# Token tiles stationary and 512 weight columns moving, in the FFNs and output projections of a three-layer network on one core

## The chip, the cores and the metric

The kernel runs on one core of a Trainium2 chip. The metric is the device time of one execution in microseconds (us). The profiled execution is a separate one, taken by the hardware profiler.

## The reference, cut to what matters

256 tokens of 1024 features go through three layers: a matrix memory mixer (mixa), a windowed attention mixer (mixb) and a state-space mixer (ssd). There are five FFNs of 2816 hidden columns: before and after mixa, before and after mixb, and after ssd. All is float32.

```
def rms_norm(x, g):
    y = xf * lax.rsqrt(jnp.mean(xf * xf, axis=-1, keepdims=True) + EPS)
    return y * g
def swiglu(x, w_in, w_out):
    gate, up = jnp.split(x @ w_in, 2, axis=-1)
    return (jax.nn.silu(gate) * up) @ w_out
mem_kv = rms_norm(mem, mem_norm_g) @ mem_w_kv
for i in range(2):
    x = x + 0.5 * swiglu(rms_norm(x, ffn1_norm_g[i]), ffn1_w_in[i], ffn1_w_out[i])
    proj = rms_norm(x, mix_norm_g[i]) @ w_in
    x = x + concat(token_mixer(proj), memory_heads(proj)) @ w_out
    x = x + 0.5 * swiglu(rms_norm(x, ffn2_norm_g[i]), ffn2_w_in[i], ffn2_w_out[i])
h = x + hybrid_mixer(rmsnorm(x, norm_mix_w))          # ends with merged @ w_o
h = h + (silu(hn @ w_gate) * (hn @ w_up)) @ w_down    # hn = rmsnorm(h, norm_ffn_w)
return rmsnorm(h, final_norm_w)
```

## The kernel before, in words

**Units of weights.** Every weight matrix comes in units of 1 MB (128 partitions x 2048 elements). A g unit is 8 k-tiles (128 input features each) of 256 output columns. A d unit is 2 k-tiles (256 input rows) of 1024 output columns. Three slots (RING) hold the units in turn. SP's queue loads unit u into w_raw when VectorE has split unit u-3 (`load`). ScalarE rounds it to float32r, w_hi (`round_`, L553), when TensorE has used unit u-3 (w_used). VectorE writes the remainder w_lo = w_raw - w_hi (`split`, L966). Activations are held as such a pair too (xg_hi and xg_lo, y_hi and y_lo), and every product is made in three passes: hi x hi, hi x lo, lo x hi.

**Matmuls.** In `block_passes` (L1676 to 1678) a 128x128 block of weights is the stationary operand and the 256 tokens are the moving one. The output is one of the 128-row blocks of features, by token. A unit has 48 such matmuls. A g unit fills one PSUM bank, (4, 5 or 6 in turn, `bank`), and a d unit adds into banks 0 to 3, which stay open over a whole FFN or projection.

**The FFN.** 11 steps (NI) of 256 hidden columns. A step is three units: g of gate, g of up, d of the step before. VectorE takes gate and up out of their banks and scales them by rstd, a row of the 256 tokens' 1/rms held on all partitions (`evac`, L1038). ScalarE makes the silu (L605), VectorE the product (L1054), ScalarE and VectorE its hi and lo (L609, L1058), which are the moving operand of the next d unit. The middle steps are in a hardware loop, two a turn.

**The residual and the norms.** x is held by feature: 8 tiles of 128 features x 256 tokens. The last d unit of a stage frees the banks 0 to 3 in order. VectorE adds them to x (L993), ScalarE scales x by the next norm's gain and rounds it (xg_hi, L575), VectorE makes xg_lo (L975), two tiles at a time, and the first g unit of the next stage takes them k-tile by k-tile. ScalarE squares x (L564), GpSimd adds the squares (L502), and two float32 matmuls with a matrix of ones bring the sum of each token on all partitions (`stat`, L1715 and 1716). The root (`token_root`) is Ln and Exp on ScalarE and a step of refinement on VectorE (L1017 to 1027), on 128x256 tiles. The root is applied only when a product is taken out of its bank. ScalarE loads a table of functions before it (ACT_TABLE_LOAD) and another one after it, for the silu.

**The ends.** mem and x come in by token and are turned by 16 transposes each (`turn`, L1723). At the end x times the final gain is turned back (L2134), and 32 records of matmuls with one moving column give the sums of squares (L2139).

**Order of the work.** Each engine has its own list, written out by hand, and waits on semaphores. In one engine's list an operation that waits holds all behind it. Of an FFN's entrance VectorE's list is: norm, split(u+2), split(u+3), token_root, evac of gate, product; u is the first unit of the FFN.

Of the kernel before, what the change touches and what calls it, by code (L numbers as in the profile page):

```python
# [17 lines left out]
F32 = mybir.dt.float32  # L18
# [6 lines left out]
P = 128  # L25
T = 256
# [33 lines left out]
def plan_units():  # L60
# [7 lines left out]
    ffn = "gg" + "ggd" * (NI - 1) + "d"  # L68
# [23 lines left out]
def build(nc, a, out, known=None):  # L92
# [6 lines left out]
    with ExitStack() as ctx:  # L99
# [10 lines left out]
        x = sb("x", [P, DT, T])  # L110
# [5 lines left out]
        rs_v = sb("rs_v", [P, T])  # L116
        rs_y = sb("rs_y", [P, T])
        rs_t = sb("rs_t", [P, T])
# [32 lines left out]
        sq = tiles(KB(0, 8), 512)  # L151
        gate_s, up_s = KB(8, 2), KB(10, 2)
        xin = tiles(KB(16, 8), D)
        memin = tiles(KB(24, 8), D)
        x_gain = tiles(KB(8, 8))
        fin_r, fin_v, fin_t = small[:, 0:2], small[:, 2:4], small[:, 4:6]
        mem_t = tiles(KB(8, 8))
        yout = tiles(KB(16, 8), D)
# [12 lines left out]
        turned = sem("turned")  # L171
        x_new = sem("x_new")
        xh_ready, xl_ready = sem("xh_ready"), sem("xl_ready")
        squared, sq_summed, stat_done = sem("squared"), sem("sq_summed"), sem("stat_done")
        rs_vec, rs_act = sem("rs_vec"), sem("rs_act")
        ffn_silu, ffn_h, ffn_hh, ffn_hl = (sem(n) for n in ("ffn_silu", "ffn_h", "ffn_hh", "ffn_hl"))
# [3 lines left out]
        def g_src(w, c):  # L180

            return w.rearrange("(k p) c -> p k c", p=P)[:, :, bass.ds(c, 256)]

        def d_src(w, r):

            return w[bass.ds(r, 256), :].rearrange("(k p) c -> p k c", p=P)

        FFNS = [(a["ffn1_w_in"][0], a["ffn1_w_out"][0]), (a["ffn2_w_in"][0], a["ffn2_w_out"][0]),
                (a["ffn1_w_in"][1], a["ffn1_w_out"][1]), (a["ffn2_w_in"][1], a["ffn2_w_out"][1]), None]

        def ffn_src(f, kind, i):

            if f == 4:
                w = {"g": a["w_gate_2"][0], "u": a["w_up_2"][0], "d": a["w_down_2"][0]}[kind]
                return d_src(w, i * 256) if kind == "d" else g_src(w, i * 256)
            w_in, w_out = FFNS[f]
            if kind == "d":
                return d_src(w_out, i * 256)
            return g_src(w_in, i * 256 + (FF if kind == "u" else 0))
# [23 lines left out]
        vector("final", r128(a["final_norm_w_2"]), 8)  # L223
# [13 lines left out]
        def col(name, k=0):  # L237
# [8 lines left out]
                  ("final", "final", 1.0)]  # L246
        LAST = ([p[0] for p in PHASES if p[0].startswith("ffn")] or [""])[-1]
        norm_of = {p[0]: (n, p[1], p[2]) for n, p in enumerate(PHASES)}

# [92 lines left out]
        def _(sp):  # L342
# [4 lines left out]
            def load(u, src, i=0):  # L347
# [5 lines left out]
                sp.dma_start(w_raw[:, u % RING, :].rearrange("p (k c) -> p k c", k=src.shape[1]),  # L353
                             src).then_inc(w_landed[u % RING], 16)

            def ffn(f):
                u = U[f"ffn{f}"]
                load(u, ffn_src(f, "g", 0))
                load(u + 1, ffn_src(f, "u", 0))
                for i in (1, 2):  # L360
                    load(u + 3 * i - 1, ffn_src(f, "g", i))
                    load(u + 3 * i, ffn_src(f, "u", i))
                    load(u + 3 * i + 1, ffn_src(f, "d", i - 1))
                with sp.Fori(0, (NI - 3) // 2) as n:
                    for j in range(2):
                        i, v = 3 + j, u + 8 + 3 * j
                        load(v, ffn_src(f, "g", 2 * n + i), n)
                        load(v + 1, ffn_src(f, "u", 2 * n + i), n)
                        load(v + 2, ffn_src(f, "d", 2 * n + i - 1), n)
                load(u + 3 * NI - 1, ffn_src(f, "d", NI - 1))  # L370
# [14 lines left out]
            def mem():  # L385
                for j in range(3):
                    load(U["mem"] + j, g_src(a["mem_w_kv"], 256 * j))
                sp.dma_start(xin, a["x"][0].rearrange("(k p) d -> p k d", p=P)).then_inc(x_loaded, 16)
# [45 lines left out]
            for c in range(4):  # L434
                if c % 2:
                    sp.wait_ge(act_done, act_.at(f"out {c}"))
                else:
                    sp.wait_ge(vec_done, vec.at(f"out {c}"))
                tt, f = c // 2, slice(512 * (c % 2), 512 * (c % 2) + 512)
# [5 lines left out]
        def _(pool):  # L445
# [49 lines left out]
            def norm(n):  # L495

                pool.wait_ge(squared, 4 * n + 2)
                for c in range(1, 4):
                    if c > 1:
                        pool.wait_ge(squared, 4 * n + c + 1)  # L500
                        pool.wait_ge(sq_summed, 3 * n + c - 1)
                    pool.tensor_tensor(sq[:, 0], sq[:, 0], sq[:, c], ALU.add).then_inc(sq_summed, 1)  # L502

# [32 lines left out]
            for name, _, _ in PHASES[:-1]:  # L536
                norm(norm_of[name][0])
# [5 lines left out]
        def _(act):  # L543
            roots = [0]

            def round_(u, i=0):
# [3 lines left out]
                act.wait_ge(w_landed[u % RING], 16 * (u // RING + 1) + 32 * i)  # L550
# [8 lines left out]
            def norm(n, gain, split=True):  # L559
                src = x if n else mem_t  # L560

                def squares():
                    for c in range(4):
                        act.activation(sq[:, c], src[:, 2 * c:2 * c + 2], ACT.Square).then_inc(squared, 1)  # L564

                if n == 1:
                    act.wait_ge(stat_done, 1)
                    act.wait_ge(x_new, 8)
                    squares()
                    act.wait_ge(w_used, U["ffn0"])  # L570
                for c in range(4):
                    act.wait_ge(x_new, 4 * n + c + 1)
                    if split:
                        for k in (2 * c, 2 * c + 1):
                            act.activation(xg_hi[:, k], src[:, k], ACT.Identity, scale=col(gain, k)).then_inc(xh_ready, 1)  # L575
                if n == 0:
                    round_(1)
                if n != 1:
                    squares()
# [11 lines left out]
            def ffn(f, n, gain):  # L591
                u = U[f"ffn{f}"]
                norm(n, gain)
                round_(u + 2)
                round_(u + 3)
                if f == 0:
# [3 lines left out]
                root(rs_y[:, :], rs_v[:, :])  # L600
                act.preload_act_table_set(SETS["silu"])

                def silu(v, i, it=0):
                    evacuated(v, it)
                    act.activation(gate_s, gate_s, ACT.Silu).then_inc(ffn_silu, 1)  # L605

                def product(i, p):
                    act.wait_ge(ffn_h, NI * nth[f] + i + 1)
                    act.activation(y_hi[:, 2 * p:2 * p + 2], tiles(up_s), ACT.Copy).then_inc(ffn_hh, 1)  # L609

                def step(g, i, p, it=0):
                    round_(g + 2, it)
                    silu(g, i, it)
                    round_(g + 3, it)
                    product(i, p)
                    round_(g + 4, it)

# [1552 lines left out]
```

## Time and profile before

| | |
|---|---|
| median of 3 runs | 1721.25 us (1720.28 to 1721.38) |
| profiled execution | span 1719.2 us, 31086 instructions |
| TensorE (PE) busy | 1652.2 us |
| VectorE (DVE) busy | 1089.0 us |
| ScalarE (ACT) busy | 792.4 us |
| GpSimd (POOL) busy | 182.1 us |
| mean granted TensorE clock | 0.989 of full speed |
| HBM | 275.01 MB read, 161 GB/s over the span |

For the profiled execution no time beside its span is given. PE is a matmul, PEld a load of the stationary operand. A record's length of a matmul includes its way through the array, so in a stream records overlap, and the distance of their starts is what a matmul costs. A float32 matmul stands in the trace as two records, a float32r one and a transpose as one.

How the rows below are to be read. The timeline: start in us, length in us (for "x10" from the first start to the last end of ten records), engine, line, operation, out<-in, shape, and in brackets idle time before and what ended it. The windows: the stretch, its length, busy us and records of PE, PEld, DVE, ACT and POOL, then the granted clock (1.00 is 2.4 GHz, 0.50 is 1.2 GHz), the busy share of the DMA engines and GB/s. The groups of instructions by line: busy us in all, mean ns of one, and idle time before them with its releaser.

### The profile page before, as it was taken

The page shows a single profiled execution, that of the slowest core. Times are in us where ns is not written, and L with a number is a line of the kernel's source. Part 1 is how long each engine was busy: PE and PEld are TensorE (multiplying, and loading weights), DVE is VectorE, ACT ScalarE, POOL GpSimd, SP SyncE. Part 2 cuts the span into 40 slices and gives each one's busy share as a digit, 9 for nine tenths or more (in the row PEclk, how much of TensorE's full clock was granted, in tenths as well). Part 3 has the DMA queues.
Part 4 walks back from the last instruction along what each step waited for, and adds up shares of the span by engine and source line. Part 5 has one row for each costly group of instructions (what it writes and reads, how often), then busy time and mean ns, then how long its engine had stood idle before and what let it go on. Part 6 is the DMA issues. An engine that isn't in the chain of part 4 may idle for free. (4 is left out here: it accounts for less than half of the span.)

```text
span 1719.2 us, 31086 instructions
## 1 busy us (share of the span) xinstructions
PE 1652.2 (96%) x13337; PEld 1615.0 (94%) x13337; DVE 1089.0 (63%) x1237; ACT 792.4 (46%) x892; POOL 182.1 (11%) x137
## 2 busy tenths in 40 slices
PE   6999999999999999999999999997889999999998
PEld 6999999999999999999789999996789999999998
DVE  5565566576665665556676655689777756665554
ACT  5543353455434453436556434454446534453432
POOL 2100010011000010001301000056741000010000
PEclk9999999999999999999999999998999999999999
DMA  8355555434555555555223555544224655545551
GB/s 251 124 183 184 195 153 167 137 110 154 187 196 172 194 172 184 183 179 170 92 87 118 199 186 176 190 148 141 80 76 150 204 184 182 183 151 197 172 194 49
DMA packets 218181, 277.42 MB, mean 161 GB/s; under 512 B 4972, under 2 KB 198888, under 8 KB 218088
## 3 DMA queue, kind: packets, MB, share of 16 engines
q1 hardware_dynamic: 218088, 276.08, 49.3%
q8 instruction: 71, 1.16, 0.3%
q14 instruction: 22, 0.18, 0.0%
HBM read 275.01 MB, written 1.05 MB: 161 GB/s over the span
## 5 line engine op out<-in xcount | busy, mean ns | idle before, releaser
L966 DVE TENSOR_TENSOR w_lo<-w_raw,w_hi 128x2048 fp32r<-128x2048 f32 x260 | 602.8, 2320 | 385.4 <-ACT w_hi L553 385.1
L1676 PE MATMUL ps<-xg_hi,w_hi 128*128 128x256 f32 x2888 | 830.4, 288 | 16.3 <-DVE xg_lo L975 11.9
L1677 PE MATMUL ps<-xg_lo,w_hi 128*128 128x256 f32 x2888 | 820.4, 284 | 0.0
L1678 PE MATMUL ps<-xg_hi,w_lo 128*128 128x256 f32 x2888 | 820.2, 284 | 0.0
L553 ACT ACTIVATE w_hi<-w_raw 128x2048 fp32r<-128x2048 f32 x260 | 494.6, 1905 | 190.1 <-PE ps L1678 176.2
L1676 PEld LDWEIGHTS ps<-xg_hi,w_hi 128*128 128x128 f32 x2888 | 557.5, 193 | 24.3 <-DVE w_lo L966 9.5
L1677 PEld LDWEIGHTS ps<-xg_lo,w_hi 128*128 128x128 f32 x2888 | 557.6, 193 | 0.5
L1678 PEld LDWEIGHTS ps<-xg_hi,w_lo 128*128 128x128 f32 x2888 | 557.4, 193 | 0.0
L1676 PE MATMUL ps<-y_hi,w_hi 128*128 128x256 f32 x1264 | 358.8, 284 | 4.8 <-DVE y_lo L1355 2.8
L1677 PE MATMUL ps<-y_lo,w_hi 128*128 128x256 f32 x1264 | 357.7, 283 | 0.0
L1678 PE MATMUL ps<-y_hi,w_lo 128*128 128x256 f32 x1264 | 357.6, 283 | 0.0
L1676 PEld LDWEIGHTS ps<-y_hi,w_hi 128*128 128x128 f32 x1264 | 242.6, 192 | 6.5 <-DVE y_lo L1355 3.3
L1677 PEld LDWEIGHTS ps<-y_lo,w_hi 128*128 128x128 f32 x1264 | 242.6, 192 | 0.0
L1678 PEld LDWEIGHTS ps<-y_hi,w_lo 128*128 128x128 f32 x1264 | 242.6, 192 | 0.0
L502 POOL TENSOR_TENSOR scr<-scr 128x512 f32<-128x512 f32 x27 | 54.0, 1999 | 1098.8 <-ACT scr L564 1096.2
L1038 DVE SCALAR_TENSOR_TENSOR scr<-ps,rstd 128x512 f32<-128x512 f32 x141 | 96.6, 689 | 86.4 <-PE ps L1678 86.0
L605 ACT ACTIVATE scr<-scr 128x512 f32<-128x512 f32 x55 | 34.7, 632 | 218.0 <-DVE scr L1038 218.0
L609 ACT ACTIVATE y_hi<-scr 128x512 fp32r<-128x512 f32 x55 | 34.8, 632 | 209.4 <-DVE scr L1054 209.4
L1058 DVE TENSOR_TENSOR y_lo<-scr,y_hi 128x512 fp32r<-128x512 f32 x55 | 38.1, 692 | 38.4 <-ACT y_hi L609 38.4
L1465 DVE SCALAR_TENSOR_TENSOR mem_v<-mem_k,cols,mem_v 128x255 f32<-128x255 f32 (+2 forms) x72 | 46.5, 709 | 0.0
L515 POOL TENSOR_SCALAR mem_k<-mem_k 128x512 f32<-128x512 f32 x12 | 39.9, 3326 | 47.2 <-ACT mem_k L857 47.2
L575 ACT ACTIVATE xg_hi<-x,cols 128x256 fp32r<-128x256 f32 x64 | 28.0, 500 | 31.5 <-DVE x L993 26.6
(292 smaller groups left out, 948.9 us busy)
## 6 DMA issues: line engine op xcount, KB each, us to landing
w_raw<-in_ffn_w_in_dram SPq DMA_DIRECT2D x88, 1024.0 KB, 5.1
w_raw<-in_ffn_w_out_dram SPq DMA_DIRECT2D x44, 1024.0 KB, 4.9
w_raw<-in_w_in_dram SPq DMA_DIRECT2D x41, 1024.0 KB, 5.3
w_raw<-in_a_w_in_dram SPq DMA_DIRECT2D x15, 1024.0 KB, 5.3
w_raw<-in_w_gate_dram SPq DMA_DIRECT2D x11, 1024.0 KB, 5.3
w_raw<-in_w_up_dram SPq DMA_DIRECT2D x11, 1024.0 KB, 5.3
w_raw<-in_w_down_dram SPq DMA_DIRECT2D x11, 1024.0 KB, 4.9
w_raw<-in_w_ssd_proj_dram SPq DMA_DIRECT2D x8, 1024.0 KB, 5.3
```

The lines of the kernel that those rows point to most:

```text
L502: pool.tensor_tensor(sq[:, 0], sq[:, 0], sq[:, c], ALU.add).then_inc(sq_summed, 1)
L515: pool.tensor_scalar(s_in[:, q:q + 2], s_in[:, q:q + 2], 1.0, None, ALU.add).then_inc(pool_done, pool_(f"S th {c}"))
L553: act.activation(w_hi[:, u % RING, :], w_raw[:, u % RING, :], ACT.Copy).then_inc(w_rounded, 1)
L605: act.activation(gate_s, gate_s, ACT.Silu).then_inc(ffn_silu, 1)
L609: act.activation(y_hi[:, 2 * p:2 * p + 2], tiles(up_s), ACT.Copy).then_inc(ffn_hh, 1)
L966: dve.tensor_tensor(w_lo[:, s, :], w_raw[:, s, :], w_hi[:, s, :].bitcast(F32), ALU.subtract).then_inc(w_split, 1)
L1038: dve.scalar_tensor_tensor(out=dst, in0=tiles(ps[:, bank(u), :]), scalar=scale, in1=wide(rstd[:, :] if r is None else r), op0=ALU.mult, op ...
L1058: dve.tensor_tensor(y_lo[:, 2 * p:2 * p + 2], tiles(up_s), y_hi[:, 2 * p:2 * p + 2].bitcast(F32), ALU.subtract).then_inc(ffn_hl, 1)
L1465: dve.scalar_tensor_tensor(out=s_cv[:, q + t, s:], in0=s_in[:, q + t, 0:T - s], scalar=col(f"conv_w{tap_}", conv_tile(c) + t), in1=s_cv[:, ...
L1676: pe.matmul(dst, hi, xh, start=start, stop=False, skip_group_check=True)
L1677: pe.matmul(dst, hi, xl, start=False, stop=False, skip_group_check=True)
L1678: last = pe.matmul(dst, lo, xh, start=False, stop=stop, skip_group_check=True)
```

## The change

**Operands exchanged.** In the FFNs, in both `mix*_out` projections and in w_o the stationary operand is now a 128x128 tile of tokens by features (xg or y, hi or lo), and the moving one is 512 columns of the weight unit (`row_passes`). A unit has 24 matmuls of 512 columns in place of 48 of 256. All other products stay as they were.

**Units.** A step of the FFN is still three units, but gate and up are mixed: each of the first two has 4 k-tiles, with 256 columns of gate and 256 of up side by side (`gu_src`, `gate_up`). The output [128 tokens x (256 gate, 256 up)] of the two token tiles is in banks 4 and 5. There is one such pair of banks; the next step's first unit waits for ffn_h in the first step, and in the loop comes behind a wait for it. Every unit is now loaded by two DMAs.

**Hidden values.** ScalarE makes the silu straight from the bank, scaled by rcol, the root as a column [128 tokens x 2]; VectorE makes the product from the bank with the same scale into h_s, by token. Four transposes (`hidden`) turn it into bank 6, from which hi and lo are made. `hidden(i)` stands in the middle of the d unit of step i-1 (after its second quarter), and for step 0 between the first and second unit of step 1.

**Residual.** x is held by token ([128, 2, 1024]). The d unit goes by quarters (token tile, half of the columns): (0,0), (1,0), (0,1), (1,1). At the end of a stage TensorE turns each added quarter by four transposes into two banks (`turn`), ScalarE and VectorE make xg_hi and xg_lo out of these banks. The turns of the first two quarters lie inside the last d unit, the others inside the first unit of the next stage.

**Norms.** ScalarE squares x by token tile and sums in its accumulator (`square`), the root is taken on two columns. The squares' sum on GpSimd and the two `stat` matmuls are gone. In the mixers two matmuls turn the root's columns into the row rstd (`token_row`). At the end the final gain is loaded as a row, and no transposes are made.

**Lists at the FFN's entrance.** ScalarE's: round u+1, four tiles of xg_hi, round u+2, square, four tiles, square, root, silu table, wait for the root, round u+3, silu. VectorE's: three adds, four tiles of xg_lo, last add, split(u+1), four tiles, split(u+2), token_root, split(u+3), product(0).

The diff, cut to its core:

```
-    ffn = "gg" + "ggd" * (NI - 1) + "d"
+    ffn = "d" * (3 * NI)
-        x = sb("x", [P, DT, T])
+        x = sb("x", [P, 2, D])
...
+        QUARTERS = ((0, 0), (1, 0), (0, 1), (1, 1))
+        def quarter(tt, half):
+            return ps[:, 2 * half + tt, :]
...
+            def high(n, gain, half_):
+                for k in range(4 * half_, 4 * half_ + 4):
+                    act.wait_ge(turned, 2 * n + half_ + 1)
+                    act.activation(normed_of(n)[0][:, k], block_of(n, k), ACT.Identity, scale=col(gain, k)).then_inc(xh_ready, 1)
+            def square(n, tt):
...
+                act.activation(sq_out[:, tt], (x if n else memin)[:, tt], ACT.Square, accum_out=ssq[:, tt:tt + 1]).then_inc(squared, 1)
+            def norm(n, gain, u):
+                round_(u + 1)
+                high(n, gain, 0)
+                round_(u + 2)
+                square(n, 0)
+                high(n, gain, 1)
+                square(n, 1)
...
-                root(rs_y[:, :], rs_v[:, :])
+                root(rn_y, rn_v)
                 act.preload_act_table_set(SETS["silu"])
+                act.wait_ge(rs_vec, root_.at(f"norm {n}") + 3)
+                round_(u + 3)
+                def silu(g, i, it=0):
+                    act.wait_ge(ffn_gu, NI * nth[f] + i + 1)
+                    act.activation(gate_s[:, 0], ps[:, 4, 0:256], ACT.Silu, scale=rcol[:, 0:1]).then_inc(ffn_silu, 1)
+                    act.wait_ge(w_used, g + 2 + 6 * it)
+                    act.activation(gate_s[:, 1], ps[:, 5, 0:256], ACT.Silu, scale=rcol[:, 1:2]).then_inc(ffn_silu, 1)
+                def step(g, i, p, it=0, first=False):
                     round_(g + 2, it)
+                    if first:
+                        hidden_high(0, 0)
+                    round_(g + 3, it)
                     silu(g, i, it)
                     round_(g + 4, it)
+                    hidden_high(i, p)
...
+            def norm(n, gain, factor, u):
+                for j in range(3):
+                    add(n, factor, u, j)
+                low(n, gain, 0)
+                add(n, factor, u, 3)
+                split(u + 1)
+                low(n, gain, 1)
+                split(u + 2)
...
+                token_root(n)
                 split(u + 3)
-                token_root(n)
+                def product(i):
+                    for tt in range(2):
+                        dve.wait_ge(ffn_silu, 2 * (NI * nth[f] + i) + tt + 1)
+                        dve.scalar_tensor_tensor(out=h_s[:, tt], in0=ps[:, 4 + tt, 256:512], scalar=rcol[:, tt:tt + 1], in1=gate_s[:, tt],
+                                                 op0=ALU.mult, op1=ALU.mult).then_inc(ffn_h, 1)
...
+            def row_passes(dst, xh, xl, s, at, start, stop):
+                hi, lo = w_hi[:, s, at:at + 512], w_lo[:, s, at:at + 512]
+                pe.matmul(dst, xh, hi, start=start, stop=False, skip_group_check=True)
+                pe.matmul(dst, xh, lo, start=False, stop=False, skip_group_check=True)
+                return pe.matmul(dst, xl, hi, start=False, stop=stop, skip_group_check=True)
...
+            def gate_up(u, half_, it=0, norm=None, first=None):
+                s = u % RING
+                pe.wait_ge(w_split, u + 1 + 6 * it)
+                for tt in range(2):
+                    if first is not None:
+                        pe.wait_ge(ffn_h, first + tt)
+                    for k in range(4):
+                        kt = 4 * half_ + k
+                        if norm is not None and tt == 0:
+                            pe.wait_ge(xl_ready, 8 * norm + kt + 1)
+                        tok = slice(tt * P, tt * P + P)
+                        last = row_passes(ps[:, 4 + tt, :], xg_hi[:, kt, tok], xg_lo[:, kt, tok], s, 512 * k, kt == 0, kt == 7)
+                    if half_ and tt == 0:
+                        last.then_inc(ffn_gu, 1)
+                    if norm is not None and norm > 1 and half_ == 0 and tt == 0:
+                        turn(norm, 2)
+                        turn(norm, 3)
+                last.then_inc(w_used, 1)
...
+                for j, (tt, h) in enumerate(QUARTERS):
+                    tok = slice(tt * P, tt * P + P)
                     for k in range(2):
+                        last = row_passes(quarter(tt, h), yh[:, y0 + k, tok], yl[:, y0 + k, tok], s, k * D + 512 * h,
+                                          start and k == 0, k == 1)
+                    if norm is not None and j < 3:
                         last.then_inc(acc_ready, 1)
+                    if norm is not None and norm < len(PHASES) - 1 and j in (1, 2):
+                        turn(norm, j - 1)
+                    if hidden and j == 1:
+                        hidden()
...
+                def hidden(i):
+                    pe.wait_ge(ffn_h, 2 * (NI * nth[f] + i) + 2)
+                    for fb in range(2):
+                        for tt in range(2):
+                            last = pe.transpose(ps[:, 6, fb * T + tt * P:fb * T + tt * P + P], h_s[:, tt, fb * P:fb * P + P], ident[:, :])
+                    last.then_inc(ffn_ht, 1)
```

## Rows read from the trace of the kernel before

**Rows 1.** Page, busy us and share of the span by engine:
```profile
PE 1652.2 (96%) x13337; PEld 1615.0 (94%) x13337; DVE 1089.0 (63%) x1237; ACT 792.4 (46%) x892; POOL 182.1 (11%) x137
```
**Rows 2.** Windows, all engines: inside an FFN, and the start of ssd:
```profile
500.00:550.00 50.00, 50.00 (x419) 50.00 (x418) 27.49 (x20) 20.36 (x15) 0.00 (x0) 1.00 0.56 188
1150.00:1200.00 50.00, 38.03 (x282) 36.66 (x281) 48.07 (x71) 24.86 (x35) 30.40 (x13) 0.87 0.46 146
```
**Rows 3.** Timeline (start, length) inside an FFN, PE and PEld:
```profile
456.56 0.28 PE L1676 MATMUL ps<-xg_hi,w_hi 128*128 128x256 f32 x1
456.56 0.19 PEld L1677 LDWEIGHTS ps<-xg_lo,w_hi 128*128 128x128 f32 x1
456.68 0.28 PE L1677 MATMUL ps<-xg_lo,w_hi 128*128 128x256 f32 x1
```
**Rows 4.** Timeline, PE: float32 records of 256, 512 and 1 columns:
```profile
347.05 2.32 PE L1801 MATMUL ps<-mem_k,scr 128*128 128x256 f32 x10
...
847.07 1.45 PE L1917 MATMUL ps<-scr,rotate 128*128 128x512 f32 x3
...
1709.15 3.63 PE L2139 MATMUL ps<-ones,scr 128*128 128x1 f32 x32
```
**Rows 5.** Timeline, PE, in a stretch at half clock:
```profile
14.38 0.41 PE L1676 MATMUL ps<-xg_hi,w_hi 128*128 128x256 f32 x1
14.59 0.41 PE L1677 MATMUL ps<-xg_lo,w_hi 128*128 128x256 f32 x1
```
**Rows 6.** Timeline, PE: sixteen transposes in a row:
```profile
316.31 1.91 PE L1865 MATMUL ps<-ident,scr 128*128 128x128 f32 x16
```
**Rows 7.** Groups by line: the first of the two statistic matmuls:
```profile
L1715 PE MATMUL ps<-scr,ones 128*128 128x256 f32 x18 | 5.5, 385 | 0.3 <-POOL scr L502 0.3
```
**Rows 8.** Timeline at a boundary from one FFN to the next:
```profile
595.97 1.71 ACT L575 ACTIVATE xg_hi<-x,cols 128x256 fp32r<-128x256 f32 x4 [2.96 <-DVE x L993]
...
596.48 0.28 PE L1678 MATMUL ps<-y_hi,w_lo 128*128 128x256 f32 x1
597.15 0.36 PE L1676 MATMUL ps<-xg_hi,w_hi 128*128 128x256 f32 x1 [0.39 <-DVE xg_lo L975]
...
599.31 1.66 DVE L975 SCALAR_TENSOR_TENSOR xg_lo<-x,cols,xg_hi 128x256 fp32r<-128x256 f32 x4
```
**Rows 9.** Groups by line: ScalarE's and VectorE's operations (busy, mean ns of one):
```profile
L553 ACT ACTIVATE w_hi<-w_raw 128x2048 fp32r<-128x2048 f32 x260 | 494.6, 1905 | 190.1 <-PE ps L1678 176.2 <-DMA w_raw<-in_mem_w_kv_dram 13.6
L585 ACT ACT_TABLE_LOAD x18 | 23.1, 1283 | 0.3
L587 ACT ACTIVATE scr<-scr 128x1024 f32<-128x1024 f32 x2 | 2.1, 1060 | 2.3 <-DVE scr L1017 2.3
L666 ACT ACTIVATION_READ_ACCUMULATOR scr<-ps,small 128x1 f32 x16 | 3.3, 209 | 0.0
...
L966 DVE TENSOR_TENSOR w_lo<-w_raw,w_hi 128x2048 fp32r<-128x2048 f32 x260 | 602.8, 2320 | 385.4 <-ACT w_hi L553 385.1
L1023 DVE SCALAR_TENSOR_TENSOR rs_t<-rs_t,rs_v 128x256 f32<-128x256 f32 x9 | 3.8, 424 | 0.3
```
**Rows 10.** Timeline: first and last VectorE record of a root on two columns:
```profile
1712.82 0.16 DVE L1017 TENSOR_SCALAR small<-ps 128x2 f32<-128x2 f32 x1 [4.00 <-PE ps L2139]
...
1713.88 0.16 DVE L1027 SCALAR_TENSOR_TENSOR small<-small 128x2 f32<-128x2 f32 x1
```
**Rows 11.** Windows: a stop of TensorE, and the stretches behind two stops:
```profile
20.70:23.60 2.90, 0.24 (x3) 0.04 (x1) 1.24 (x1) 0.00 (x0) 2.76 (x2) 0.99 0.99 185
23.50:26.90 3.40, 3.26 (x15) 3.26 (x16) 0.00 (x0) 0.41 (x1) 0.97 (x1) 0.50 1.10 362
...
866.80:870.00 3.20, 3.20 (x16) 2.87 (x17) 3.20 (x14) 1.88 (x4) 0.00 (x0) 0.50 0.27 104
```
**Rows 12.** Timeline: the last matmul of the last d unit, and the stores:
```profile
1705.59 0.28 PE L1678 MATMUL ps<-y_hi,w_lo 128*128 128x256 f32 x1
...
1714.86 1.83 SPq L440 DMA_DIRECT2D out_dram<-scr  x4
```

More of the change, by code:

```diff
@@ L592, in ffn @@
                 u = U[f"ffn{f}"]
[L593 to L596, printed above, removed]
+                if f:
+                    norm(n, gain, u)
+                else:
+                    for tt in range(2):
+                        square(n, tt)
+                    round_(u + 2)
                     for j in range(2):
@@ L636, in ffn @@
                     step(u + 11 + 6 * (bodies - 1), NI - 1, 0)
-                round_(u + 3 * NI + 1)
             def mem(n, gain):
                 u = U["mem"]
-                norm(n, gain)
+                act.wait_ge(vec_done, vec.at("mem gain"))
+                high(n, gain, 0)
+                round_(u + 1)
+                high(n, gain, 1)
+                for tt in range(2):
+                    square(n, tt)
                 round_(u + 2)
+                root(rn_y, rn_v)
                 round_(u + 3)
-                root(rs_y[:, :], rs_v[:, :])
-                round_(u + 4)
+                for half_ in range(2):
+                    high(n + 1, PHASES[1][1], half_)
                 for j in range(2):
@@ L1076, in step @@
                         next(extra, None)
-                evac(tiles(gate_s), u)
-                product(u, 0)
-                low(0, 0)
-                step(u + 2, 1, 1, more=f == 1)
+                product(0)
+                step(u + 2, 1, 1, more=f == 1, first=True)
                 if f == 0:
@@ L1687, in g_unit @@
                     pe.wait_ge(drained[s], fills[u] - 1 + 2 * i)
-                for n, off in enumerate(offs):
-                    for k in range(8):
-                        if norm is not None and n == 0:
-                            pe.wait_ge(xl_ready, 8 * norm + k + 1)
-                        if ready and n == 0:
-                            ready(k)
-                        last = block_passes(ps[:, b, n * T:n * T + T], s, k * 256 + off, xh[:, kt0 + k],
-                                            xl[:, kt0 + k], opens and n == 0 and k == 0, k == 7)
@@ L1696, in g_unit @@
-                last.then_inc(w_used, 1)
-            def d_unit(u, i=0, Y=None, y0=0, start=False, norm=None):
+                order = [(n, off, k) for n, off in enumerate(offs) for k in range(8)]
+                if norm is not None:
+                    order = [(n, off, k) for h in range(2) for n, off in enumerate(offs) for k in range(4 * h, 4 * h + 4)]
+                for n, off, k in order:
+                    if norm is not None and n == 0:
+                        if k == 4:
+                            turn(norm, 2)
+                            turn(norm, 3)
+                        pe.wait_ge(xl_ready, 8 * norm + k + 1)
+                    if ready and n == 0:
+                        ready(k)
+                    last = block_passes(ps[:, b, n * T:n * T + T], s, k * 256 + off, xh[:, kt0 + k],
+                                        xl[:, kt0 + k], opens and n == 0 and k == 0, k == 7)
@@ L1727, in ffn, with token_row @@
+            def token_row(n):
+                pe.wait_ge(rs_vec, root_.at(f"norm {n}") + 3)
+                for tt in range(2):
+                    last = pe.matmul(ps[:, STAT, tt * P:tt * P + P], rcol[:, tt:tt + 1].broadcast_to([P, P]), ident[:, :], start=True, stop=True)
+                last.then_inc(stat_done, 1)
             def ffn(f, n):
                 u = U[f"ffn{f}"]
-                g_unit(u, norm=n)
+                if f == 0:
+                    for v in range(u - 3, u):
+                        evacuated(v)
+                gate_up(u, 0, norm=n)
@@ L2123, in _ @@
             pe.wait_ge(mem_loaded, 16)
-            turn(memin, 0)
+            pe.wait_ge(vec_done, vec.at("mem gain"))
+            for j in range(2):
+                turn(0, j)
             for name, _, _ in PHASES:
@@ L2130, in _ @@
                     {"mem": mem, "mixa": mixa, "mixb": mixb, "ssd": ssd}[name](n)
-            for k in range(DT):
-                pe.wait_ge(vec_done, vec.at(f"x gain {k}"))
-                for tt in range(2):
-                    last = pe.transpose(ps[:, 2 * tt + k // 4, (k % 4) * P:(k % 4) * P + P], x_gain[:, k, tt * P:tt * P + P], ident[:, :])
-            last.then_inc(pe_done, pe_("out"))
-            pe.wait_ge(squared, 4 * norm_of["final"][0] + 4)
-            for tt in range(2):
-                for k in range(DT):
-                    last = pe.matmul(ps[:, STAT, tt:tt + 1], tiles(sq[:, k // 2])[:, k % 2, tt * P:tt * P + P], ones[:, 0:1],
-                                     start=k == 0, stop=k == DT - 1, skip_group_check=True)
-            last.then_inc(stat_done, 1)
     return {e: c.found for e, c in counts.items()}
```

451 lines of the change are left out of this document (209 added, 242 removed).

## The prediction, made before the change was run

> **What bounds the kernel now.** I read the busy shares first: TensorE is busy for 1652.2 us of the span of 1719.2 us, VectorE for 63% and ScalarE for 46% [rows 1]. The windows show where: in a stretch inside an FFN (500 to 550 us) TensorE is busy for all 50 us at the full clock while VectorE has 27.5 us and ScalarE 20.4 us; only the start of the last mixer (1150 to 1200 us) is a VectorE stretch, 48.1 us of 50 [rows 2]. So for an FFN the question is how densely matmuls follow each other. A matmul record lasts 284 ns, but that is its way through the array; the timeline shows the next one starting 0.12 us later, 456.56 and 456.68, and so on [rows 3]. 256 columns at 2.4 GHz are 106.7 ns, so 13.3 ns of each 120 are not streaming. Two things could be behind it, and they decide this case. Rows with one moving column settle it as far as this trace can: 32 records in 3.63 us, so (3.63 - 0.25) / 31 = 0.109 us each, with nothing to stream [rows 4]. That is the loading of 128 stationary columns. In the stream a load record starts with the matmul before it and its own matmul starts 0.12 us later [rows 3]. And at half clock, where 256 columns take 213.3 ns, the spacing is 0.21 us with no addition [rows 5]: the load is hidden there. I read 120 ns as the interval of a load, not of a matmul.
>
> **The matmuls.** The five FFNs have 33 weight units each and the output projections 6 + 6 + 4; each unit has 48 matmuls of 256 columns, so 181 x 48 = 8688, at 0.120 us 1042.6 us. After the change there are 4344 of 512 columns, each again with one load. No float32r matmul of 512 columns stands in the trace. The nearest rows are float32 passes, which stand at two array cycles a column: ten records of 256 columns in 2.32 us are (2.32 - 0.38) / 9 = 0.216 us for 512 cycles, and 512 columns take (1.45 - 0.59) / 2 = 0.43 us for 1024 [rows 4]. Both are the streaming plus 2 to 3 ns, with a load hidden in each. I take 0.216 us: 938.3 us, a gain of 104.3. Bounds: 0.2133 (streaming alone, 12 us better) and 0.240 (twice the row of now, no gain at all).
> The row for 256 columns is 120 ns [rows 3]. By the Trainium skill ("TensorE: Matmul & The Clock Gate", section "Wait — 56ns, not 53.3ns?") a warm matmul starts N/2.4 GHz plus about 2.5 ns after the last. That is 109 ns for 256 columns, against the trace, and 215.8 for 512. Were the page right for both widths, a pair would go from 218.4 to 215.8 and the edit would be worth 11 us instead of 104; the row of 120 decides against it.
>
> **Transposes that are added.** An FFN step (256 hidden columns) now has h by token and turns it back: four 128x128 transposes, 5 x 11 x 4 = 220. Sixteen of them in a row take 1.91 us, (1.91 - 0.27) / 15 = 0.109 us each [rows 6]: 24.0 us on TensorE. Lower bound the same; upper bound 0.272 us each, a record's whole length, if four alone between wide matmuls don't overlap. The residual must be turned for each norm too: 16 transposes at 7 boundaries (mem and x were turned before as well), 112 x 0.109 = 12.2 us.
> The Trainium skill ("TensorE: Matmul & The Clock Gate", section "Part 4: PE-mode transpose") gives some 275 ns for a transpose in a kernel. As a record's length the trace agrees (272 ns); as the price in a row it has 109. With 275 for all 332 the two items would be 91 us instead of 36 and the change a loss of 5; rival E below is its case here, worked out from the 272 of the row.
>
> **Norms.** The sum of squares leaves TensorE (ScalarE's accumulator makes it): 9 stages x 4 records of 256 columns in float32 x 0.216 = 7.8 us less [rows 7]. Four mixer stages get 4 records of 128 columns (broadcasting the root), 0.11 us each, 1.8 us. Net -6.0.
>
> **Boundaries.** Now TensorE stops three times at the entrance of a stage, because xg_lo comes in pairs: 596.48 to 597.15 and so on, where 0.12 would do, in all 1.6 us at each of 7 boundaries [rows 8]. In the new order the last down unit runs by quarter, and the turns of the first two quarters lie inside it. The last quarter is 6 x 0.216 = 1.3 us; in it and just after it lie the drain (0.2), two scalings on ScalarE (0.43 us apart) and one xg_lo (0.45) [rows 8]: first product about 0.4 us after the last down matmul, and then 0.65 us per k-tile against 0.43 on the other engines. So an FFN boundary stalls 0.4 us instead of 1.6 (four times: -4.8). In a mixer the second half of the k-tiles comes earlier: ScalarE first rounds a weight unit (1.9) and squares 1024 elements (1.06 + 0.21) [rows 9], and only then scales; TensorE, through with its first half and eight transposes at about 4.2 us, waits until 5.8. That makes 2.2 us in mixa and mixb, 3.2 in the last one, +2.8 in all. Net -2.
>
> **Entrance of an FFN.** Here a stall is added. Gate and up of one step fill two banks, for two token tiles, and there is no second pair. So the third unit (gate_up of step 1) can't start before product(0) has read them, and product(0) needs the root and stands behind split(u+3) in VectorE's queue. With 0 at the end of the last down unit: TensorE does unit u from 0.4 to 6.5 (24 x 0.216 and 0.87 of transposes) and u+1 until 11.7. ScalarE gets the last four k-tiles turned at 4.1 and has scaled them by 5.8; VectorE's last xg_lo is out at 6.7, then split(u+2) runs 2.3 us to 9.0. The root of two columns is 1.2 us from its first VectorE record to its last [rows 10], 10.2. ScalarE loads the silu table after its Exp (1.28 us) to about 11.0, rounds u+3 (1.9) to 12.9; VectorE splits it (2.3) to 15.2; silu is done by then, the first product takes 0.45: 15.7. TensorE stands from 11.7, 4.0 us, in four FFNs; in the first, the mem values' copies take the place of the norm, 3.6 us. Together 19.6. Behind the split wait both products, h's transposes and so the bank pair. The trace also shows what such a stop costs later: after 2.9 us with TensorE nearly idle, 3.4 us at half clock (15 matmuls in 3.4 us); the same after the stop at 864.9 [rows 11]. I charge 1.5 us each, +7.5. Bounds of this item: 0, if my order of events is too strict, and 35.
>
> **Inside the loop.** A step is 72 x 0.216 + 0.44 = 16.0 us, 17.3 now. The transposes of h come after half a down unit, 12 x 0.216 = 2.6 us behind the end of gate_up; until then silu of the second tile (0.2 + 0.45) and its product (0.45) must be done: 1.2 us, slack 1.4. ScalarE has 3 x 1.9 + 1.5 us in a step, VectorE 3 x 2.3 + 1.6 (three or four short operations, 0.42 us per 256 columns) [rows 9], so both stay below TensorE. A weight unit lands and is rounded some 4 us before it is needed; two DMAs a unit instead of one cost SP 0.4 us more of 5.3. Nothing of it reaches TensorE.
>
> **Smaller ones.** First FFN: it waits for evac of the last mem unit before it opens its banks, 0.95 us, and the mem keys' root on VectorE is closer to TensorE: +2. The chain of the windowed attention in mixb swallows some of what its out units give: +1. End: now 13.6 us lie between the last matmul (1705.59) and the end, of them 16 transposes, 32 one-column records and 1.4 us of output [rows 4, 12]. After: add 0.7, gain and square 0.9, table 1.3, root 1.2, output 1.4, the stores' issue and landing (from 1714.86 to 1719.24: 4.4) with overlap about 9.5: -4.
>
> **Sum.** -104.3 + 24.0 + 12.2 - 6.0 - 2.0 + 27.1 + 2 + 1 - 4 = -50.0. The profiled execution spans 1719.2 us; the median of the runs is 1721.25, 2.0 above. 1719.2 - 50.0 + 2.0 = 1671 us.
>
> **Rivals.**
> A. The 13.3 ns are an addition to every matmul: 226.7 ns, +46.5 us, 1718. For it: all 12,000 records have it. Against: rows 4 and 5, where it is 2 to 3 ns or none. 7%.
> B. The slower side: float32r columns are fed at 0.469 ns each, so 512 take 240 ns. Then 104.3 is gone, and the transposes, stops and turns remain: 1775 us. It decides from 227.5 ns a matmul on (50 / 4344 above 216). For it: 120 / 256, and neither the half-clock rows nor the float32 passes (0.84 ns a column) are fast enough to show such a limit. Against: the records with one column take 0.109 us with nothing to feed, so a load explains the row without it. 4%.
> C. h is late at its transposes in every step; the place is the product of the second tile behind split in VectorE's queue. 0.4 us a step makes 22 us, 1693; to undo the gain it would take 0.9. For it: product stands behind a wait that ends with the unit. Against: the slack of 1.4. 6%.
> D. The entrance stall is hidden: -25 us, 1646. 7%.
> E. Four transposes between wide matmuls cost 272 ns each: 332 x 0.163 = +54, 1725. 2%.
> Mine has 74%, with its own range 1656 to 1688. The range 1650 to 1712 leaves out B, E, most of A and half of D, about 18%. A change within 0.2% can't be told from none here: faster 0.90, same 0.04, slower 0.06.
>
> **What would show it.** In the timeline of an FFN the starts of wide matmuls 0.216 us apart (0.227 is A, 0.240 is B); groups of four transposes at 0.11 with no idle ahead; a wait of TensorE for the product (ffn_h) of about 4 us once in each FFN, followed by 3.4 us at half clock; the first wait at a boundary below 0.5 us for FFNs and one of 1.6 in mixers; the tail at 9.5 us. An FFN of 33 units should go from 190 us to about 182. If waits for h stand in every step, or if the spacing isn't 0.216, the sum is wrong.

## The result, and the profile after

The changed kernel takes 1710.51 us (median of 4 runs, 1709.77 to 1711.49), the kernel before 1720.82 in the same comparison: ratio 0.9943, 95% interval 0.9931 to 0.9956. The direction is the forecast one, and the gain is clear of the noise, but of 50 us there came 10. The profiled execution spans 1708.1 us, 11.1 less than before.

The page of the changed kernel, beside [rows 1] (its matmul records fell from 13337 to 9257):

```profile
span 1708.1 us, 23310 instructions
PE 1627.5 (95%) x9257; PEld 1412.0 (83%) x9257; DVE 1000.0 (59%) x1175; ACT 806.1 (47%) x951; POOL 128.1 (7%) x110
```

TensorE is still the engine that bounds the kernel. How dense its matmuls are is read from the timeline inside an FFN, beside [rows 3], and from the windows, beside [rows 2]:

```profile
700.04 0.39 PE L1717 MATMUL ps<-w_hi,xg_hi 128*128 128x512 f32 x1
700.26 0.39 PE L1718 MATMUL ps<-w_lo,xg_hi 128*128 128x512 f32 x1
700.49 0.39 PE L1719 MATMUL ps<-w_hi,xg_lo 128*128 128x512 f32 x1
700.72 0.39 PE L1717 MATMUL ps<-w_hi,xg_hi 128*128 128x512 f32 x1
```

```profile
700.00:750.00 50.00, 50.00 (x227) 41.36 (x227) 25.06 (x18) 21.13 (x19) 0.00 (x0) 1.00 0.56 188
```

Three matmuls take 0.68 us from start to start: 0.227 us each, not 0.216. TensorE has no gap, and the load records fill 41.4 us of the 50, where they filled all 50 before.

The group of four transposes of h (an FFN's first one), and the entrance of the same FFN, where TensorE waits for the first product. The timeline, PE first, then what the other engines do in that time:

```profile
602.14 0.39 PE L1719 MATMUL ps<-w_hi,xg_lo 128*128 128x512 f32 x1
605.85 0.76 PE L1717 MATMUL ps<-w_hi,xg_hi 128*128 128x512 f32 x1 [3.32 <-DVE scr L1088]
...
614.15 0.60 PE L1812 MATMUL ps<-ident,scr 128*128 128x128 f32 x4
614.50 0.48 PE L1717 MATMUL ps<-w_hi,xg_hi 128*128 128x512 f32 x1
```

```profile
599.04 0.17 DVE L1045 TENSOR_SCALAR norms<-norms 128x2 f32<-128x2 f32 x1
599.70 1.28 ACT L627 ACT_TABLE_LOAD   x1
600.99 1.92 ACT L575 ACTIVATE w_hi<-w_raw 128x2048 fp32r<-128x2048 f32 x1
602.82 0.45 ACT L633 ACTIVATE scr<-ps,norms 128x256 f32<-128x256 f32 x1
603.01 2.29 DVE L1002 TENSOR_TENSOR w_lo<-w_raw,w_hi 128x2048 fp32r<-128x2048 f32 x1 [2.75 <-ACT w_hi L575]
605.22 0.87 DVE L1088 SCALAR_TENSOR_TENSOR scr<-ps,norms,scr 128x256 f32<-128x256 f32 x2
```

This is the chain that the prediction wrote out, link by link: root, table, rounding of u+3, its split, and only then the products, though the silu of the first token tile was ready at 603.3 and that of the second at 603.6. The windows of the stop and of what follows (the granted clock is the third number from the end):

```profile
602.20:605.80 3.60, 0.33 (x2) 0.00 (x0) 2.79 (x3) 3.23 (x4) 0.00 (x0) 0.87 0.42 147
605.80:611.60 5.80, 5.75 (x14) 4.52 (x15) 2.49 (x2) 0.00 (x0) 0.00 (x0) 0.50 0.88 292
```

14 matmuls take the time of 25: behind a stop of 3.5 us some 2.8 are lost (15 matmuls take from 605.85 to 612.06). [rows 11] had the same kind of thing, 3.4 us at half clock behind a stop of 2.9; here the stretch is twice as long.

Starts of the first matmul of a unit give the price of each stage (worked out from the timeline). A unit of gate and up takes 5.44 us (5.76 before), a down unit with its transposes 5.93, so a step 16.81 instead of 17.28. But a whole FFN of 33 units hardly changed: ffn1, ffn2 and ffn3 (after mixa, before and after mixb) took 193.7, 193.0 and 192.3 us before and take 190.7, 193.5 and 193.4 now, where the prediction had about 182.

### The profile page after: what moved, and what is told of

The parts are those of the page before. It is cut to its first block and busy times, and to the rows that moved or that the text cites. A ratio compares the mean times of both kernels' runs of the same rounds, so it can differ in the third digit from the quotient of the medians.

```text
span 1708.1 us, 23310 instructions
## 1 busy us (share of the span) xinstructions
PE 1627.5 (95%) x9257; PEld 1412.0 (83%) x9257; DVE 1000.0 (59%) x1175; ACT 806.1 (47%) x951; POOL 128.1 (7%) x110
## 5 line engine op out<-in xcount | busy, mean ns | idle before, releaser
L1717 PE MATMUL ps<-w_hi,xg_hi 128*128 128x512 f32 x912 | 361.3, 396 | 18.4 <-DVE scr L1088 16.8
L1718 PE MATMUL ps<-w_lo,xg_hi 128*128 128x512 f32 x912 | 358.6, 393 | 0.0
L1719 PE MATMUL ps<-w_hi,xg_lo 128*128 128x512 f32 x912 | 358.6, 393 | 0.0
L1709 PE MATMUL ps<-xg_hi,w_hi 128*128 128x256 f32 x1000 | 290.4, 290 | 6.6 <-DVE xg_lo L1010 4.6
L1710 PE MATMUL ps<-xg_lo,w_hi 128*128 128x256 f32 x1000 | 284.9, 285 | 0.0
L1711 PE MATMUL ps<-xg_hi,w_lo 128*128 128x256 f32 x1000 | 284.7, 285 | 0.0
L1717 PE MATMUL ps<-w_hi,y_hi 128*128 128x512 f32 x536 | 215.7, 402 | 3.0 <-DVE y_lo L1386 3.0
L1709 PEld LDWEIGHTS ps<-xg_hi,w_hi 128*128 128x128 f32 x1000 | 193.6, 194 | 11.2 <-DVE xg_lo L1010 5.3
L1710 PEld LDWEIGHTS ps<-xg_lo,w_hi 128*128 128x128 f32 x1000 | 193.8, 194 | 0.3
L1711 PEld LDWEIGHTS ps<-xg_hi,w_lo 128*128 128x128 f32 x1000 | 193.7, 194 | 0.0
```

Of the source, the lines that this page charges most:

```text
L1709: pe.matmul(dst, hi, xh, start=start, stop=False, skip_group_check=True)
L1710: pe.matmul(dst, hi, xl, start=False, stop=False, skip_group_check=True)
L1711: last = pe.matmul(dst, lo, xh, start=False, stop=stop, skip_group_check=True)
L1717: pe.matmul(dst, xh, hi, start=start, stop=False, skip_group_check=True)
L1718: pe.matmul(dst, xh, lo, start=False, stop=False, skip_group_check=True)
L1719: return pe.matmul(dst, xl, hi, start=False, stop=stop, skip_group_check=True)
```

## The experiments

In the comparisons of e2, e3 and e4 the kernel before had a median of 1719.43 us, in those of e5 and e7 1719.70, against 1720.82 in that of the change. Differences to the changed kernel (1710.51) are therefore good to a microsecond or so; each ratio is to the kernel before of its own comparison.

**e1_streams: the disputed cost by itself.** Fifteen series of 24 matmuls, each like the first of these lines (xr and wr are float32r copies, xb and wb bfloat16 ones, x and w float32):

```
for j in range(24):
    pe.matmul(ps[:, j % 4, :], xr_tile(j), wr_tile(j, 512), start=True, stop=True)
# others: accumulating in one bank; 384, 256, 128 columns; one stationary tile only;
# 64 stationary columns; bfloat16; float32; with ScalarE and VectorE streaming
```

> This kernel leaves the whole network out: it loads a piece of x and of one weight matrix, makes float32r and bfloat16 copies, and runs series of 24 matmuls on 128x128 stationary tiles, each series on a line of its own, so its time is no time of the network. Read is the distance of starts at the full clock. Theory 1, a fixed addition to each float32r matmul (13.4 ns as in the network): 512 columns 227 ns, 384 173, 256 120, 128 about 67 or the interval of a load if that is longer (112 to 120); accumulation into one bank, the same stationary tile again, and 64 stationary columns all stay at 227; bfloat16 216 and 109 at 512 and 256. Theory 2, the company of ScalarE and VectorE makes the addition: all bare float32r series of 512 columns at 216, and 227 only in the last two series, where both engines stream over SBUF. Theory 3, the part of a load that isn't hidden: 227 with 128 stationary columns, about 220 with 64.

The timeline of PE. In order: 512 columns, 384, 256, 128; 64 stationary columns; bfloat16 with 512 and 256 columns; ScalarE and VectorE streaming (L109):

```profile
23.84 5.60 PE L84 MATMUL ps<-wr,xr 128*128 128x512 f32 x24
34.72 4.35 PE L88 MATMUL ps<-wr,xr 128*128 128x384 f32 x24
38.90 3.03 PE L90 MATMUL ps<-wr,xr 128*128 128x256 f32 x24
41.77 2.80 PE L92 MATMUL ps<-wr,xr 128*128 128x128 f32 x24
49.94 5.69 PE L96 MATMUL ps<-wr,xr 128*64 128x512 f32 x24
55.47 5.35 PE L98 MATMUL ps<-wb,xb 128*128 128x512 bf16 x24
60.66 2.78 PE L100 MATMUL ps<-wb,xb 128*128 128x256 bf16 x24
77.84 5.63 PE L109 MATMUL ps<-wr,xr 128*128 128x512 f32 x24
```

Less the last record's own length and over 23: (5.60 - 0.39) / 23 = 226.6 ns for 512 columns, 174 for 384, 120 for 256. Each is the streaming at 2.4 GHz plus 13.3 (384: 14). 128 columns come out at 0.110 us, where streaming and addition would make 67 ns; rows with one column had 0.109 [rows 4], so I take this for the floor that the load sets. The bfloat16 series have 216 and 109. With 64 stationary columns nothing is saved (230). One stationary tile all the time has a median of 227 (512 columns) and 120 (256), and accumulation into one bank 227 too. In the series L109 ScalarE and VectorE stream over SBUF all the time: 228; in L84 and L86 both are silent: 226.6. So theory 1 holds, theories 2 and 3 fall: the addition is there in a kernel with nothing else in it, doesn't hang on the load, and belongs to float32r.

**e6_streams2: what carries it.** The same frame, other operands:

```
stat(j)[0:64], mov(j, 512)[0:64]          # and 0:32
stat(j), one_column.broadcast_to([128, 512])
stat(j), mov(j, 512)[:, 0::2]             # 256 columns, stride two
stat(j), mov(j, 320)
6 x wide matmul, 4 x transpose, eight times over
float32r and bfloat16 in turn
```

> Again no network, only series of 24 matmuls (float32r, 512 columns where nothing else is said), for what carries the addition of 13.3 ns: 64 and 32 rows (partitions) in place of 128; a moving operand that is one column repeated; a stationary operand that is one column repeated; 256 columns at a stride of two; 320 columns; the same moving tile each time; six wide matmuls and four transposes in turn; float32r and bfloat16 in turn. If the addition belongs to the start of a float32r matmul: 227 ns in all wide series, 120 at stride two, 147 for 320 columns, and 227 + 216 for the pair with bfloat16. If it belongs to reading a tile from memory: less with the repeated column or with few partitions. If it belongs to float32r's load of the stationary tile: gone or moved in the pair, 216 + 227 with the order of the two exchanged, and the same sum. Six wide matmuls and four transposes should take 6 x 0.227 + 4 x 0.109 = 1.80 us, and 1.85 if a group of transposes has an edge of its own, as the network's 0.49 us a group suggests.

The timeline of PE: the moving operand one column repeated (eight records at full clock); the stationary operand one column repeated; stride two; 320 columns; the group of six wide matmuls and four transposes, twice:

```profile
41.30 1.89 PE L89 MATMUL ps<-wr,xr 128*128 128x512 f32 x8
43.67 5.72 PE L91 MATMUL ps<-wr,xr 128*128 128x512 f32 x24
49.23 5.61 PE L93 MATMUL ps<-wr,xr 128*128 128x256 f32 x24
54.66 3.70 PE L95 MATMUL ps<-wr,xr 128*128 128x320 f32 x24
70.87 1.64 PE L100 MATMUL ps<-wr,xr 128*128 128x512 f32 x6
72.34 0.60 PE L102 MATMUL ps<-ident,x 128*128 128x128 f32 x4
72.70 1.63 PE L100 MATMUL ps<-wr,xr 128*128 128x512 f32 x6
```

With one moving column repeated the 512-column matmul takes (1.89 - 0.38) / 7 = 0.216 us: the addition is gone. With one stationary column repeated it stays, (5.72 - 0.39) / 23 = 232 ns. With fewer rows it stays (the starts' median distance is 227 ns with 64 and with 32), and with the same moving tile each time as well (median 227). 320 columns take 147 ns, on the same line. And 256 columns at stride two cost what 512 neighbouring ones cost, (5.61 - 0.39) / 23 = 227 ns. So the addition belongs to the moving tile, most likely to its reading (a repeated column also has all values equal, and no run keeps the two apart), and the "start of a float32r matmul" of my expectation is refuted in that form. The pair with bfloat16 took 460 ns, against 443 expected, and doesn't tell the theories apart. The group of six and four repeats every 1.83 us, between my two numbers: the transposes are worth 0.47 with their edges.

**e2_narrow: the width undone, all else kept.**

```
-    hi, lo = w_hi[:, s, at:at + 512], w_lo[:, s, at:at + 512]
-    pe.matmul(dst, xh, hi, ...); pe.matmul(dst, xh, lo, ...); return pe.matmul(dst, xl, hi, ...)
+    for c in (0, 256):
+        hi, lo, o = w_hi[:, s, at + c:at + c + 256], w_lo[:, s, at + c:at + c + 256], dst[:, c:c + 256]
+        pe.matmul(o, xh, hi, ...); pe.matmul(o, xh, lo, ...); last = pe.matmul(o, xl, hi, ...)
```

> The changed kernel with each 512-column matmul made as two of 256; all else (token tiles stationary, transposes, norms, lists) stays. Theory 1 (fixed addition): 4344 more matmuls, each pair 240 instead of 227 ns, so +58 us: about 1768 us, and the rest of the change then costs some 47 us against the kernel before. If narrow matmuls with tokens stationary were cheaper than 120 ns (the load of an activation tile being quicker than one of weights), the rise would be well below 58.

1754.41 us, ratio to before 1.0203 (1.0186 to 1.0220): 44 to 45 us over the changed kernel, not 58. The matmuls do stand at 0.12 again, tokens stationary or not:

```profile
700.11 0.28 PE L1718 MATMUL ps<-w_hi,xg_hi 128*128 128x256 f32 x1
700.23 0.28 PE L1719 MATMUL ps<-w_lo,xg_hi 128*128 128x256 f32 x1
```

A unit is back at 5.76 us, so the 58 are there (181 units x 0.32). What is missing by the same reading: the entrance stop is 3.0 us instead of 3.5, since TensorE comes later to the same product; a group of h's transposes adds 0.43 instead of 0.49; and stretches at half clock cost less: both widths take 213 ns per 256 columns there, and the FFNs of this trace have 13.7 us of them instead of 23.9. The sum of these is not closed to the microsecond. The run shows the main thing: without the width the rest of the change is a loss of 2%.

**e3_entry: the entrance stop removed.** In the FFN's lists:

```
 ScalarE:  wait for the root
-          round_(u + 3)
           silu(u, 0)
+          round_(u + 3)
 VectorE:  token_root(n)
-          split(u + 3)
           product(0)
+          split(u + 3)
```

> The changed kernel with the two lists at an FFN's entrance changed: ScalarE rounds unit u+3 after the first silu, VectorE splits it after the first product. Theory of the entrance stall: TensorE's wait for the product goes from 3.5 us to under 1 in five FFNs (-14 to -17 us), and the stretches at half clock behind it (6.8, 6.8, 6.8 and 3.4 us) go too, worth 0.2 us for each wide matmul in them (-8 to -10): 1684 to 1689 us. Rival: the wait only moves, to unit u+3, whose split is now 3 us later: TensorE waits there, and the time stays within 5 us of 1710.

1681.42 us, ratio 0.9780 (0.9764 to 0.9797), 28 to 29 us under the changed kernel and 3 to 8 better than expected. The list of TensorE's waits (in all, times, longest) begins with the product in the changed kernel:

```profile
PE ps L1717 <- DVE scr L1088: 16.8, 5, 3.6
```

In e3_entry that wait is gone from the list, which now begins with one in the last mixer and two at the start of the kernel:

```profile
PE ps L2140 <- ACT scr L898: 13.8, 5, 11.2
PE ps L2205 <- DMA scr<-in_mem_norm_g_dram: 6.5, 1, 6.5
PE ps L1709 <- DVE y_lo L1010: 6.4, 2, 4.9
```

No stretch at half clock stands in an FFN any more. Window of the same FFN's entrance:

```profile
590.00:600.00 10.00, 10.00 (x47) 8.27 (x46) 6.20 (x8) 7.04 (x8) 0.00 (x0) 1.00 0.48 134
```

From unit start to unit start the five FFNs are 6.4, 3.5, 6.3, 6.2 and 5.0 us shorter, 27.4 in all; 5 x 3.48 = 17.4 of them are the stop, 10.0 the half clock (ffn1 had no such stretch and lost the stop alone). The rival (the wait moves to unit u+3) is refuted.

**e4_twice: h's transposes doubled.**

```
-    for fb in range(2):
+    for fb in (0, 1, 0, 1):
```

> The changed kernel with each group of four transposes of h made twice (220 more transposes). Theory: they cost 0.109 us each in TensorE's row, +24 us, 1734. Rival E of the prediction (0.272 each when alone between wide matmuls): +24 as well for the doubled ones if they overlap each other, but over 40 if they do not. Rival: they lie in time that TensorE would wait in anyway: under +5.

1729.56 us, ratio 1.0070 (1.0053 to 1.0087): 19 to 20 us over the changed kernel. In the steady part a down unit goes from 5.93 to 6.34 us, 0.10 a transpose, 22 us in 55 steps. The profiled execution is 17.7 us longer than the changed kernel's; it also has fewer stretches at half clock in the FFNs (13.7 us instead of 23.9), which fits the difference. Neither cheap in a shadow nor 0.272.

**e7_one_turn: one transpose of four**, on the base of e3_entry:

```
-    for fb in range(2):
-        for tt in range(2):
+    for fb in range(1):
+        for tt in range(1):
```

> The kernel of e3_entry with one transpose of h in place of four in each FFN step; three quarters of h are not turned, and what the d units take in their place is old, so the output isn't the reference's. Theory: three transposes at 0.109 us, 55 times, -18 us: 1663. Rival, a fixed price of a group (its change of operand kind on TensorE): most of it stays and the gain is below 10.

1665.41 us, ratio 0.9683 (0.9668 to 0.9697), 16.0 under e3_entry; by the spans 17.7. A down unit is 5.61 us: one transpose adds 0.17, four 0.49. So 0.11 each and 0.05 to 0.06 for the edge of a group.

**e5_early: the turns earlier in the mixers**, on the base of e3_entry; the better version that the experiments point to:

```
 for n, off, k in order:           # n: output block, k: k-tile
+    if norm is not None and len(offs) > 1 and n == 1 and k == 0:
+        turn(norm, 2); turn(norm, 3)
     if norm is not None and n == 0:
-        if k == 4:
+        if k == 4 and len(offs) == 1:
             turn(norm, 2); turn(norm, 3)
```

> The kernel of e3_entry, and in the first unit of mixa and mixb the turns of the last two quarters come after four k-tiles of the first output block instead of after four k-tiles of both, so that the other block's four k-tiles (12 matmuls, 1.44 us) lie in TensorE's wait for the second half of xg_lo. Theory: TensorE's stops of 1.72 us there go below 0.5, -2.5 us in all: about 1679 us. Rival: the wait is set by ScalarE's square before the scaling and not by the turns; then the stop stays and nothing is gained.

1679.59 us, ratio 0.9768 (0.9755 to 0.9782). Against e3_entry (0.9780) the intervals overlap, so the times don't tell the two kernels apart. The traces do: mixa takes 2.5 us less than in e3_entry and mixb 2.3 (1.2 less than in the changed kernel), and the 1.72 us between the last turn's start and the next matmul's are gone; the widest distance left there is 0.55 us. The rival (the scaling sets the wait, nothing is gained) is refuted in mixa and mixb. Changed kernel, then e5_early, timeline of PE at mixa's turns:

```profile
245.18 1.04 PE L1787 MATMUL ps<-ident,x 128*128 128x128 f32 x8
247.66 0.38 PE L1709 MATMUL ps<-xg_hi,w_hi 128*128 128x256 f32 x1 [1.45 <-DVE xg_lo L1010]
```

```profile
237.56 1.04 PE L1790 MATMUL ps<-ident,x 128*128 128x128 f32 x8
238.36 0.37 PE L1709 MATMUL ps<-xg_hi,w_hi 128*128 128x256 f32 x1
```

One thing was not tried: VectorE waits for two tiles of xg_hi before it makes the first xg_lo (at most one scaling on ScalarE, some 0.4 us, at each boundary). Both tiles are in one PSUM bank, and without the wait the two engines would read it unordered.

## Why the prediction was wrong, step by step

**The matmuls: here it failed.** The step is "I read 120 ns as the interval of a load, not of a matmul", and with it "I take 0.216 us: 938.3 us, a gain of 104.3". Measured: 226.6 ns, 5.44 us a unit, 181 x 0.32 = 57.9 us. The 13.3 ns are an addition to every float32r matmul at the full clock, whatever its load; e1 shows them without the network, and e2 shows what the width is worth in it. That is rival A to the tenth (226.7), to which I gave 7%, and 46 of the 50 us hung on it. Each number was read rightly and none was of the same kind as the question:
- The float32 rows of [rows 4] have no addition, but they move a column every 0.83 ns. So does the half clock of [rows 5]. e1 and e6 show the addition where distinct float32r columns move at 0.42 ns each. I had noted for rival B that these rows are too slow to show a limit of that sort, and used the same rows against rival A.
- Matmuls with one column start every 0.109 us, and e1 has the same floor for float32r (0.110 at 128 columns). If that is the load's interval, it still lies 10 ns below 120, and I took the two for one number.
- A direct row for float32r at another width would have settled it, and the trace had none. The honest reading was two cases of similar weight, 0.216 and 0.227, hence some 1671 or 1718, and a range that holds both.

**h's transposes.** 24.0 forecast, 27 measured (55 x 0.49). The 0.109 of [rows 6] is the price inside a row of transposes; a group has an edge of 0.05 to 0.06. Rival E is refuted.

**The entrance of an FFN.** 27.1 forecast, 27.4 measured (e3). The mechanism was right; the sum is so close because two misses cancel: stops of 3.5 instead of 4.0 us (17.4 instead of 19.6), half clock 10.0 instead of 7.5. Rival D is refuted.

**Inside the loop.** No wait for h stands in TensorE's list beyond 0.9 us once; rival C is refuted, and with 0.227 a matmul rival B too (it asked for 0.240).

**Boundaries, norms, first FFN, mixb and end.** Forecast together +3.2 (12.2 - 6.0 - 2.0 + 2 + 1 - 4), and what is left of the measured difference is -11.1 + 57.9 - 27.0 - 27.4 = -7.6. At an FFN boundary the start after the last down matmul comes at 0.54 us where 0.23 would do, a stop of 0.3 for the forecast 0.4:

```profile
589.95 0.40 PE L1719 MATMUL ps<-w_hi,y_lo 128*128 128x512 f32 x1
590.49 0.47 PE L1717 MATMUL ps<-w_hi,xg_hi 128*128 128x512 f32 x1
```

In the mixers it was 1.45 (the row above) instead of 1.6. The end was 4.3 us shorter, as forecast (-4): last matmul at 1698.78, stores from 1703.54, against 1705.59 and 1714.86 of [rows 12]:

```profile
1698.78 0.39 PE L1719 MATMUL ps<-w_hi,y_lo 128*128 128x512 f32 x1
...
1703.54 1.82 SPq L472 DMA_DIRECT2D out_dram<-scr  x4
```

Most of the 10.8 us that are better lie at the start and in the first FFN. The mem stage was 2.7 us shorter where I had put nothing: TensorE used to stop 2.7 us for the small vectors' DMA, and now it comes later to them and stops 0.5. The first FFN lost 6.0 us over its 33 units of 5.76 before, and with e3's lists 3.6 over its new units and groups; I had forecast that it would lose 2.9 more than before (2 of stall, 1.7 of turns, less 0.9 for the two statistic matmuls), so some 5 us are better there. ffn1 to ffn3 lost 3.6, 2.9 and 2.2 us before, the statistic matmuls included, and lose 2.3 each with e3's lists, the turns included; that is near the forecast. No experiment took these items apart.

With rival A's price and all else as forecast the sum is 1718, and the measured 1710.5 is 7 below. So one term carries the miss, 46 us; of the others the transposes were 3.0 dearer and the last group 10.8 cheaper. That group is also why there is a gain to be seen: with its forecast value the change would come out at -57.9 + 27.0 + 27.4 + 3.2 = -0.3 us. The 1710.5 lies within the outer range (1650 to 1712) by this alone, and not by the merit of the forecast; it is luck, and so is the right direction.

## What to carry to other kernels

A price read at one width and kind must not be carried to another through rows of a third kind: before resting 100 us on an interval, list which limits the analogous row is fast enough to show, and keep every case that it can't exclude at full weight. When operands are exchanged, count the transposes per step against the gain per step: here 0.96 us a step were gained and 0.49 paid back. A one-time wait at a loop's entrance deserves a look at the lists of the other engines: two lines moved (weight preparation for later behind the first product) were worth nearly three times what the whole change brought.

## What the runs showed of the hardware that was not expected

- A float32r matmul with distinct moving columns costs columns / 2.4 GHz plus 13.3 ns: 226.6 ns (512), 147 (320), 174 (384, 14 over), 120 (256). With one moving column repeated it is 216, and bfloat16 has 216 and 109 for 512 and 256 columns.
- At half clock nothing is added: 213 ns for 256 and 427 for 512 columns.
- 256 float32r columns at a stride of two cost 227 ns, as much as 512 neighbouring ones. That would fit a reading in pairs of words, one pair every 0.83 ns, with a start that only a reader at its limit can't hide; this explanation is inferred from the intervals and no run shows it directly.
- A stop of 3.5 us was followed by half clock for 3.4 or 6.8 us in four of five FFNs of the changed kernel, and by none in the fifth. Behind the stop 1.5 to 2.9 us were lost each time in the four, 10.0 in all.
